# Banded attention of a two-block transformer kernel: values stationary, three heads moving, exponentials normed on GpSimd, five steps of lag

## The chip, the cores and the metric

The kernel runs on one core of a Trainium2 chip. Time is the device time of one execution in microseconds (us). The engines are TensorE (PE, with its weight loads apart as PEld), VectorE (DVE), ScalarE (ACT), GpSimd (POOL) and SyncE (SP, which only issues the loads of weights). They run side by side, each through its own instructions in their written order, and wait for each other on semaphores that the kernel sets by hand.

## The reference

Two blocks of two layers each, on 512 tokens of width 1024, in float32. The change lies in the first block, in the banded ("sliding window") attention, six query heads and two key/value heads of 64:

```python
def swa_mixer(q, k, v, q_gain, k_gain, sinks, rel_bias):
    ...
    s = jnp.einsum('bnqhgd,bnkhd->bnhgqk', qb, kb).astype(jnp.float32) * (HEAD_DIM ** -0.5)
    ...
    s = jnp.where(mask[None, :, None, None], s + bias[None, None], -jnp.inf)
    sk = sinks.astype(jnp.float32).reshape(1, 1, SWA_KV_HEADS, SWA_GROUP, 1, 1)
    lse = jnp.logaddexp(jax.nn.logsumexp(s, axis=-1, keepdims=True), sk)
    p = jnp.exp(s - lse)
    o = jnp.einsum('bnhgqk,bnkhd->bnqhgd', p.astype(v.dtype), vb)
    return o.reshape(B, S, SWA_Q_DIM)
...
        mixed = jnp.concatenate([out_a, out_b, out_c], axis=-1)
        x = x + mixed @ w_out[l]
```

A token block of 128 queries sees its own 128 keys and the 128 before (the first block only its own). `out_a` is this attention, `out_b` a pooling mixer, `out_c` full attention from latents ("mla"). The second block has two more attentions, "fox" and "nsa".

## The kernel before

Activations lie transposed (channels on partitions, 512 tokens in the row). Every weight is cut into an upper and a lower fp32r part: ACT writes the upper (`Wh`, L1520), DVE the lower by a subtraction (`Wl`, L2283), and a linear step is three 512-column matmuls (`three`, L667 to L669), called a triple here. Units of weights are cut two ahead of their use.

Each engine's program is written as one main line of linear stages and several side generators. After a piece of a linear stage the main line calls `tick()`, which lets every open side do one step. All engines make the same calls, so a step of a side stands at the same place of the main line on each. The order is the one written; nothing schedules it.

The banded attention of layer l is the side `swa_side`. It runs in the ticks of `outa{l}` (two halves of 20 ticks: five k tiles for four output tiles, one triple each). The first ticks go to the end of the mla attention, the last 32 to this side. After both halves `out0{l}` multiplies the banded output by its three k tiles; its first matmul waits for that output (`window_part`).

The 24 items are (token block t, head h), in `attend`. Of item i, step i takes the scores (two matmuls, L1209 and L1210, keys moving in 256 columns, for t = 0 in 128). On DVE one instruction adds the bias and takes the maximum (L2542), a second negates it (L2545); ACT takes the exponential with its sum (L1675). Step i + 3 turns the exponentials by PE transposes (L888), which ACT copies out (L1693). Step i + 5 mixes: the turned exponentials are the stationary tile and 64 columns of plain float32 values move (L903). After six heads of a block, DVE divides 384 columns by the sums at once (L2584), PE turns them back (L920), ACT writes the upper part `Hh` (L1582) and DVE the lower `Hl` (L2353). For the sink, DVE and ACT handle six heads in one small instruction each (L2555, L1688, L2569, L2573).

`mixing`, used by fox and nsa, is the other form. Every exponential is multiplied by its own inverted sum on GpSimd (`normalise`, L3455) before it is turned; the turned tile is split into an upper part by ACT (L1582, `PTh`) and a lower one by DVE (L2353, `PTl`); the values, upper and lower side by side in 128 columns, are stationary and several items move at once, `PTh` against both parts (L979) and `PTl` against the upper (L980). The output comes out transposed; its rows 64 to 127 have to be added to its rows 0 to 63, by an ACT copy and a DVE addition (L2081, L3123 in nsa).

PSUM has eight banks, handed out in turn by `Banks`; a new use waits until its reader has drained the last one. `outa` holds four of them. ACT runs `turn`, then `head`, then the output's copies in a step; DVE `head`, then `turn`.

Of the kernel before, what the change touches and what calls it, by code (L numbers as in the profile page):

```python
# [17 lines left out]
P = 128  # L18
S = 512
# [152 lines left out]
class Memory:  # L172


    def __init__(self, nc, ctx):
# [67 lines left out]
        self.DT = area("DT", [2, S], 19328)  # L243
        self.WSQ = area("WSQ", [2048], 6784)
# [95 lines left out]
class Signals:  # L340


    def __init__(self, nc, ctx):
# [299 lines left out]
def tensor_program(pe, M, G, K, plan):  # L643
# [225 lines left out]
    def attend(tag, items, H, scores, values, outer=True, first_mix=None, group=None):  # L869
# [73 lines left out]
    def mixing(B, scores, values, first_mix=None, group=None, extra=None, need=None, tail=6):  # L943
# [47 lines left out]
        for i in range(n + tail):  # L991
# [4 lines left out]
            c = B.ended(i - 5)  # L996
            if need and c is not None and B.closes(c) and items[i - 5][0] in PAIRS[1]:
# [36 lines left out]

    ex = Count(G.ex)
# [144 lines left out]
    for l in range(DEPTH):  # L1180
# [45 lines left out]
        def swa_values():  # L1226
            pe.wait_ge(*K.drained(f"vt{l}"))
# [274 lines left out]
def scalar_program(sc, M, G, K, plan, a):  # L1502
# [160 lines left out]
    def attend(tag, items, H, to, grouped=False):  # L1663
# [3 lines left out]
        def head(i):  # L1667
# [6 lines left out]
            if kind == "swa":  # L1674
                sc.activation(pb, pb, ACT.Exp, bias=nm, accum_out=sm).then_inc(*ex.up())  # L1675
            else:
                if i >= 4:
                    sc.wait_ge(*K.full(f"{tag} t{i - 4}"))
                sc.activation(pb, b[:, 0:w], ACT.Exp, bias=nm, accum_out=sm).then_inc(*K.empties(name))

        def turn(i):
# [3 lines left out]
            if kind == "swa" and h == H - 1:  # L1685
                x = M.STT[:, 3, t, 0:H]
                sc.wait_ge(*sink.due())
                sc.activation(x, x, ACT.Exp).then_inc(G.sink_ex, 1)  # L1688
# [1913 lines left out]
```

## Time and profile before

| | us |
|---|---|
| three runs | 2717.89, 2719.95, 2719.98 (median 2719.95) |
| the profiled execution | 2718.81 |
| its span | 2717.0 |
| PE busy | 2674.8 (98%) |
| DVE, ACT, POOL busy | 1521.7 (56%), 1135.1 (42%), 210.0 (8%) |

The span is the time from the first to the last instruction recorded; 1.8 us lie around it. The granted TensorE clock was full throughout (0.999). The chain of work that ended last lies on PE for 89% of the span and on DVE for 5%. The busy shares are averages over the whole program and say little of a stage: the banded attention stage runs from 147.6 to 195.2 us in layer 0 and from 697.6 to 745.2 us in layer 1.

### The profile page before, as it was taken

The numbers are of one execution on the slowest core, as the hardware profiler recorded it, in microseconds if no ns is written. First come the engines' busy times: TensorE is split into PE (matmuls) and PEld (weight loads), VectorE is DVE, ScalarE is ACT, GpSimd is POOL, SyncE is SP. The second block draws the span as 40 slices with busy tenths as digits, with TensorE's granted clock in tenths as the row PEclk, the third lists the DMA queues.
The fourth block names the chain that finished last, engine by engine and source line by source line (L and its number), as shares of the span: only waits on it lengthen the run. The fifth ranks groups of instructions, "written<-read, shape, count | busy, mean of one in ns | idle before, by whom it ended". The sixth has DMA issues, their size and how long they took to land.

```text
span 2717.0 us, 34704 instructions
## 1 busy us (share of the span) xinstructions
PE 2674.8 (98%) x13449; PEld 2217.3 (82%) x13449; DVE 1521.7 (56%) x2678; ACT 1135.1 (42%) x2055; POOL 210.0 (8%) x323
## 2 busy tenths in 40 slices
PE   8999999999999999999999999999999999999999
PEld 7788888887888888878877888888878778888887
DVE  7756444467564444676776653343677776643343
ACT  4644222236542222455655343242465655342232
POOL 5200000002000000021122000000020121000000
PEclk9999999999999999999999999999999999999999
DMA  5113232321132333333311333333333212323332
GB/s 146 36 42 103 93 101 93 101 81 58 34 101 96 98 97 98 93 101 89 114 48 40 98 96 93 101 94 98 109 88 105 79 40 63 104 91 101 93 101 86
DMA packets 192279, 237.70 MB, mean 87 GB/s; under 512 B 12674, under 2 KB 145764, under 8 KB 192116
## 3 DMA queue, kind: packets, MB, share of 16 engines
q1 hardware_dynamic: 188852, 228.04, 27.9%
q0 software_dynamic: 2256, 5.52, 1.0%
q8 instruction: 108, 1.77, 0.3%
q10 hardware_dynamic: 1008, 1.92, 0.2%
q14 instruction: 55, 0.45, 0.0%
HBM read 227.05 MB, written 2.11 MB: 84 GB/s over the span
## 4 chain that ended last, share of the span: by engine, by line
PE 89%; DVE 5%; ACT 2%; POOL 1%; issue 1%; DMA 0%; SPq 0%; ACTq 0%; DVEq 0%; POOLq 0%
PE bank L667 26%; PE bank L669 26%; PE bank L668 26%; PE bank L958 2%; PE bank L903 1%; PE bank L979 1%; PE bank L980 1%; PE bank L1022 1%; PE bank L1021 1%; DVE Wl L2283 1%; PE bank L1223 1%; PE bank L888 1%; PE bank L1032 1%; PE bank L1421 1%; PE bank L1017 0%
## 5 line engine op out<-in xcount | busy, mean ns | idle before, releaser
L2283 DVE TENSOR_TENSOR Wl<-RAW,Wh 128x1024 fp32r<-128x1024 f32 (+4 forms) x434 | 511.5, 1201 | 326.0 <-ACT Wh L1520 325.1
L1520 ACT ACTIVATE Wh<-RAW 128x1024 fp32r<-128x1024 f32 (+4 forms) x434 | 438.1, 1032 | 397.6 <-PE bank L669 392.4
L667 PE MATMUL bank<-Hh,Wh 128*128 128x512 f32 x1104 | 448.3, 406 | 2.2 <-DVE Hl L2353 1.5
L669 PE MATMUL bank<-Hh,Wl 128*128 128x512 f32 x1104 | 431.7, 391 | 0.0
L668 PE MATMUL bank<-Hl,Wh 128*128 128x512 f32 x1104 | 431.0, 390 | 0.0
L667 PE MATMUL bank<-HA,Wh 128*128 128x512 f32 x704 | 274.2, 390 | 0.0
L669 PE MATMUL bank<-HA,Wl 128*128 128x512 f32 x704 | 273.9, 389 | 0.0
L668 PE MATMUL bank<-HA,Wh 128*128 128x512 f32 x704 | 273.9, 389 | 0.0
L669 PEld LDWEIGHTS bank<-Hh,Wl 128*128 128x128 f32 x1104 | 207.2, 188 | 45.0
L667 PEld LDWEIGHTS bank<-Hh,Wh 128*128 128x128 f32 x1104 | 208.3, 189 | 40.6 <-issue 4.8
L668 PE MATMUL bank<-A,Wh 128*128 128x512 f32 x608 | 236.5, 389 | 0.0
L667 PE MATMUL bank<-A,Wh 128*128 128x512 f32 x608 | 236.5, 389 | 0.0
L669 PE MATMUL bank<-A,Wl 128*128 128x512 f32 x608 | 236.5, 389 | 0.0
L668 PEld LDWEIGHTS bank<-Hl,Wh 128*128 128x128 f32 x1104 | 208.1, 188 | 33.6
L669 PEld LDWEIGHTS bank<-HA,Wl 128*128 128x128 f32 x704 | 132.1, 188 | 27.5
L668 PEld LDWEIGHTS bank<-HA,Wh 128*128 128x128 f32 x704 | 132.2, 188 | 27.3
L667 PEld LDWEIGHTS bank<-HA,Wh 128*128 128x128 f32 x704 | 132.1, 188 | 27.3
L2452 DVE TENSOR_TENSOR XT<-bank,XT 128x512 f32<-128x512 f32 x112 | 77.1, 690 | 121.6 <-PE bank L669 121.0
L1738 ACT ACTIVATE P<-bank,STT 128x384 f32<-128x384 f32 (+1 forms) x192 | 101.2, 527 | 96.7 <-DVE STT L2639 95.8
L667 PE MATMUL bank<-Wh,Hh 128*128 128x512 f32 (+3 forms) x384 | 139.4, 363 | 2.2 <-DVE Wl L2283 2.2
L2353 DVE TENSOR_TENSOR A<-TMP,A 128x512 fp32r<-128x512 f32 x108 | 74.8, 693 | 117.9 <-ACT A L1933 87.2
L669 PE MATMUL bank<-Wh,Hl 128*128 128x512 f32 (+3 forms) x384 | 134.6, 350 | 0.0
(408 smaller groups left out, 4711.3 us busy)
## 6 DMA issues: line engine op xcount, KB each, us to landing
RAW<-in_w_up_dram SPq DMA_DIRECT2D x108, 512.0 KB, 3.7
RAW<-in_w_down_dram SPq DMA_DIRECT2D x108, 512.0 KB, 3.7
RAW<-in_w_in_dram SPq DMA_DIRECT2D x86, 512.0 KB, 3.7
RAW<-in_w_gate_dram SPq DMA_DIRECT2D x44, 512.0 KB, 3.7
RAW<-in_w_out_dram SPq DMA_DIRECT2D x28, 512.0 KB, 3.7
RAW<-in_cmp_w_dram SPq DMA_DIRECT2D x16, 512.0 KB, 3.9
RAW<-in_w_o_fox_dram SPq DMA_DIRECT2D x8, 512.0 KB, 4.5
RAW<-in_w_o_nsa_dram SPq DMA_DIRECT2D x8, 512.0 KB, 3.5
```

The costliest lines, as they stand in the source:

```text
L667: pe.matmul(o, sh, mh, start=first, stop=False)
L668: pe.matmul(o, sh, ml, start=False, stop=False)
L669: return pe.matmul(o, sl, mh, start=False, stop=last)
L888: x = pe.transpose(b[:, k * P:(k + 1) * P], M.PB[:, i % 4, k * P:(k + 1) * P], ident)
L903: x = pe.matmul(b[:, h * 64:(h + 1) * 64], M.PT[:, i % 3, k * P:(k + 1) * P], values(g, h, kb[k]), start=k == 0, stop=k == len(kb) - 1)
L958: x = pe.transpose(b[:, k * P:(k + 1) * P], e[:, k * P:(k + 1) * P], ident)
L979: pe.matmul(b[:, c:c + w], v, ph, start=B.opens(n) and k == 0, stop=False, skip_group_check=True)
L1520: sc.activation(M.Wh[:, v % NHL, 0:n], M.RAW[:, v % NRAW, 0:n], ACT.Copy).then_inc(G.w_hi, 1)
L1738: sc.activation(e, M.bank[K.of(name)][:, 0:e.shape[1]], ACT.Exp, bias=M.STT[:, 0, t, h:h + 1], accum_out=M.STT[:, 1, t, h:h + 1]).then_inc ...
L2283: ve.tensor_tensor(M.Wl[:, v % NRAW, 0:n], M.RAW[:, v % NRAW, 0:n], M.Wh[:, v % NHL, 0:n].bitcast(F32), ALU.subtract).then_inc(G.w_lo, 1)
L2353: return ve.tensor_tensor(lo, src, h.bitcast(F32), ALU.subtract)
L2452: ve.tensor_tensor(M.XT[:, k, :], M.bank[K.of(name)][:, :], M.XT[:, k, :], ALU.add).then_inc(*K.empties(name))
```

## The change

The banded attention leaves `attend` for `mixing`. Its items are grouped in eight trios, one (t, key/value head g) with three heads each. `mixing` gets a lag of 5 (3 elsewhere) and a tail of 8: item i is turned in step i + 5, a trio is mixed in the step i + 7 of its last item, and its finish, after the second trio of a block, is in i + 8. New operations: the upper and lower values `VS` once a layer; in each item's step the sink's exponential on ACT, the sum and its inverse on DVE, a multiplication on GpSimd, and the lower part of the turned tile on DVE; for each trio two ACT copies and two DVE additions into `OSW`, and for each block one ACT copy (`Hh`) and one DVE subtraction (`Hl`) from it. The transposes back (L920) and the division (L2584) go.

```diff
+        self.VS = area("VS", [NT, 2, P], 11904, F32R)
+        self.OSW = area("OSW", [3, S], 14976)
...
+def swa_bundles(l):
+    trios = [[(t, g, 3 * g + x) for x in range(3)] for pair in PAIRS for g in range(2) for t in pair]
+    return Bundles(f"swa{l}", trios, lambda t, g, h: f"{t}{g}", lambda t, g, h: h % 3 * P)
...
 tensor_program, mixing (scalar and vector alike)
-            if 0 <= i - 3 < n:
-                turn(i - 3)
+            if 0 <= i - lag < n:
+                turn(i - lag)
...
-            yield from attend(f"swa{l}", softmax_items(6), 6, swa_scores, lambda g, h, k: M.V1[:, k, 64 * (h // 3):64 * (h // 3) + 64],
-                              first_mix=swa_values)
+            yield from mixing(swa_bundles(l), swa_scores, lambda t, g, h, k: M.VS[:, k, g, :], swa_values, tail=8, lag=5)
...
             if k == 0:
-                for t in range(NT):
-                    pe.wait_ge(*K.drained(f"swa{l} x{t}0"))
+                pe.wait_ge(G.swa_lo, NT * l + NT)
...
 scalar_program, mixing, head
+            if banded:
+                nm = M.STT[:, 0, t, h:h + 1]
+                sc.activation(e, e, ACT.Exp, bias=nm, accum_out=M.STT[:, 1, t, h:h + 1]).then_inc(*ex.up())
+                sc.activation(M.STT[:, 3, t, h:h + 1], M.SNK[:, 6 * int(tag[3]) + h:6 * int(tag[3]) + h + 1], ACT.Exp, bias=nm).then_inc(G.sink_ex, 1)
+                return
...
+            sc.activation(M.VS[:, :, :, 0:64], M.V1[:, :, :].rearrange("p s (g d) -> p s g d", d=64), ACT.Copy).then_inc(*hi.up())
+            yield from mixing(swa_bundles(l), take=swa_take, finish=swa_out, tail=8, lag=5)
+
+        def swa_take(t, g, h):
+            o = f"swa{l} o{t}{g}"
+            sc.wait_ge(*K.full(o))
+            halves, b = trio(g, M.bank[K.of(o)])
+            for r0, x, j in halves:
+                i = sc.activation(M.OSW[r0:r0 + 64, j, t * P:(t + 1) * P], b[0:64, x, :], ACT.Copy)
+            i.then_inc(G.whole, 1)
+
+        def swa_out(t, g, h):
+            if g:
+                for x in range(2):
+                    sc.wait_ge(*K.drained(f"swa{l} o{t}{x}"))
+                sc.activation(M.Hh[:, 0:3, t * P:(t + 1) * P], M.OSW[:, :, t * P:(t + 1) * P], ACT.Copy).then_inc(*hi.up())
...
 vector_program, mixing
+            if banded:
+                if B.freed_by(i) is not None:
+                    ve.wait_ge(*K.full(f"{tag} t{B.freed_by(i)}"))
+                e, top, sk = B.exps(M, i), M.STT[:, 2, t, h:h + 1], 6 * int(tag[3]) + h
+                ve.tensor_tensor_reduce(e, M.bank[K.of(name)][:, 0:e.shape[1]], M.BIAS[:, h, (0 if t else P):256], 1.0, M.SNK[:, sk:sk + 1],
+                                        ALU.add, ALU.max, top).then_inc(*K.empties(name))
+                ve.wait_ge(*K.drained(name))
+                ve.tensor_scalar(M.STT[:, 0, t, h:h + 1], top, -1.0, None, ALU.mult).then_inc(*mx.up())
+                return
...
+            if banded:
+                total = M.STT[:, 1, t, h:h + 1]
+                ve.wait_ge(*ex.due())
+                ve.wait_ge(*sink_ex.due())
+                ve.tensor_tensor(total, total, M.STT[:, 3, t, h:h + 1], ALU.add).then_inc(*own.up())
+                ve.wait_ge(*own.now())
...
+        def swa_sum(t, g, h):
+            o = f"swa{l} o{t}{g}"
+            ve.wait_ge(*whole.due())
+            halves, b = trio(g, M.bank[K.of(o)])
+            for r0, x, j in halves:
+                y = M.OSW[r0:r0 + 64, j, t * P:(t + 1) * P]
+                i = ve.tensor_tensor(y, y, b[64:128, x, :], ALU.add)
+            i.then_inc(*K.empties(o))
+
+        def swa_out(t, g, h):
+            if g:
+                q = slice(t * P, (t + 1) * P)
+                lower(M.Hl[:, 0:3, q], M.OSW[:, :, q], M.Hh[:, 0:3, q]).then_inc(G.swa_lo, 1)
...
 gpsimd_program
+        normalise(swa_bundles(l), lambda t, g, h: M.ONE[:, 0:1])
```

DVE before, inside layer 0's stage, where the output of a block is divided (line numbers of each kernel's own; `ISA` is the bias-and-maximum instruction, its second row the read of its accumulator; `TMP`, later `P`, are the exponentials):

```order
L2542 ISA TMP_55,STT_69<-bank,BIAS_73,SS_71 128x256 [waits bank7_full,bank4_full]
L2542 ISA STT_69 128x1
L2545 TENSOR_SCALAR STT_69<-STT_69 128x1 [waits bank4_drained]
L2584 TENSOR_TENSOR OS_56<-bank,STT_69 128x384 [waits bank6_full,vector_own]
L2542 ISA TMP_55,STT_69<-bank,BIAS_73,SS_71 128x256 [waits bank7_full]
L2542 ISA STT_69 128x1
L2545 TENSOR_SCALAR STT_69<-STT_69 128x1 [waits bank7_drained]
```

DVE in the changed kernel, one step in which a trio's output is added up, and the start of the next:

```order
L2650 ISA P_9_57,STT_69<-bank,BIAS_73,SS_71 128x256 [waits bank1_full,bank3_full]
L2650 ISA STT_69 128x1
L2653 TENSOR_SCALAR STT_69<-STT_69 128x1 [waits bank3_drained]
L2663 TENSOR_TENSOR STT_69<-STT_69 128x1 [waits sink_exp_made,score_exp_made]
L2667 RECIPROCAL STT_69<-STT_69 128x1 [waits vector_own]
L2376 TENSOR_TENSOR PT_59<-bank,PT_58 128x128 [waits part_hi_made]
L3012 TENSOR_TENSOR OSW_98<-OSW_98,bank 64x128 [waits mixed_values_copied]
L3012 TENSOR_TENSOR OSW_98<-OSW_98,bank 64x2x128
L2650 ISA P_9_57,STT_69<-bank,BIAS_73,SS_71 128x256 [waits bank6_full,bank1_full]
```

Where three instructions stood for an item, six stand now, and two more for each trio behind a wait for ACT (`mixed_values_copied`).

ACT in the changed kernel, a step that takes a trio's output (copies of `OSW`) and a step with a block's `Hh`:

```order
L1740 ACTIVATE P_9_57,STT_69<-P_9_57,STT_69 128x256 [waits score_max_made]
L1741 ACTIVATE STT_69<-SS_71,STT_69 128x1
L2014 ACTIVATE OSW_98<-bank 64x128 [waits bank3_full]
L2014 ACTIVATE OSW_98<-bank 64x2x128
L1590 ACTIVATE PT_58<-bank 128x2x128 [waits bank0_full]
L1740 ACTIVATE P_9_57,STT_69<-P_9_57,STT_69 128x256 [waits score_max_made]
L1741 ACTIVATE STT_69<-SS_71,STT_69 128x1
L2021 ACTIVATE Hh_50<-OSW_98 128x3x128 [waits bank3_drained,bank6_drained]
```

The copies stand behind the exponential of the same step, which waits for DVE's maximum of that step.

PE before, the end of one item of a 256-key block and the next one's mixing:

```order
L888 MATMUL bank<-CST_61,TMP_55 128x128 [waits score_exp_made,bank6_drained]
L888 MATMUL bank<-CST_61,TMP_55 128x128
L1209 MATMUL bank<-KH_90,QP_89 128x256 [waits bank5_drained]
L1210 MATMUL bank<-KL_91,QP_89 128x256
L903 MATMUL bank<-V_36_84,TMP_55 128x64 [waits bank6_drained]
L903 MATMUL bank<-V_36_84,TMP_55 128x64
L667 MATMUL bank<-Hh_50,Wh_54 128x512
```

and in the changed kernel, a step that mixes a trio:

```order
L970 MATMUL bank<-CST_61,P_9_57 128x128 [waits score_exp_normed,bank0_drained]
L970 MATMUL bank<-CST_61,P_9_57 128x128
L1219 MATMUL bank<-KH_90,QP_89 128x256 [waits bank6_drained]
L1220 MATMUL bank<-KL_91,QP_89 128x256
L991 MATMUL bank<-PT_58,VS_97 128x384 [waits bank6_drained,bank0_drained,bank3_drained,bank1_drained]
L992 MATMUL bank<-PT_59,VS_97 64x384
L991 MATMUL bank<-PT_58,VS_97 128x384
L992 MATMUL bank<-PT_59,VS_97 64x384
L682 MATMUL bank<-Hh_50,Wh_54 128x512
```

Two steps in three have no mixing; the third has four matmuls of 384 columns.

## Rows read from the trace of the kernel before

**Rows 1.** Windows of the stage: us, busy (count) of PE, PEld, DVE, ACT, POOL, clock, DMA
```profile
147.60:153.20 5.60, 5.21 (x29) 4.11 (x28) 4.31 (x16) 2.89 (x10) 0.00 (x0) 1.00 0.13 47
153.20:185.00 31.80, 30.35 (x198) 25.56 (x198) 19.91 (x77) 19.84 (x67) 0.00 (x0) 1.00 0.13 43
185.00:195.20 10.20, 9.51 (x58) 7.83 (x56) 5.28 (x14) 4.99 (x12) 0.00 (x0) 1.00 0.09 26
...
697.60:745.20 47.60, 45.08 (x283) 37.48 (x282) 29.54 (x105) 27.73 (x88) 0.00 (x0) 1.00 0.12 40
```
**Rows 2.** Timeline of PE, one item: start, duration, what [idle before, releaser]
```profile
171.39 0.38 PE L888 MATMUL bank<-CST,TMP 128*128 128x128 f32 x2
...
171.84 0.55 PE L903 MATMUL bank<-V,TMP 128*128 128x64 f32 x4
172.21 0.47 PE L667 MATMUL bank<-Hh,Wh 128*128 128x512 f32 x1
...
172.98 0.38 PE L888 MATMUL bank<-CST,TMP 128*128 128x128 f32 x2
```
**Rows 3.** Timeline of PE, a block's output turned back, and the stage's end
```profile
191.61 0.49 PE L920 MATMUL bank<-CST,OS 128*128 128x128 f32 x3
191.85 0.47 PE L667 MATMUL bank<-Hh,Wh 128*128 128x512 f32 x1
...
195.24 0.47 PE L667 MATMUL bank<-Hh,Wh 128*128 128x512 f32 x1 [0.73 <-DVE Hl L2353]
```
**Rows 4.** Timeline of PE in fox: a 384-column fp32r matmul and the next
```profile
1181.06 0.34 PE L1022 MATMUL bank<-KAl,QA 128*128 128x384 f32 x1
1181.23 0.34 PE L1024 MATMUL bank<-CR,SEL 96*128 96x384 bf16 x1
```
**Rows 5.** Timeline of DVE in the stage: one item's head, back to back
```profile
151.55 0.48 DVE L2542 CUSTOM_DVE_ANT_0 TMP<-bank,BIAS,SS 128x256 f32<-128x256 f32 x1
...
152.07 0.15 DVE L2545 TENSOR_SCALAR STT<-STT 128x1 f32<-128x1 f32 x1
152.15 0.34 DVE L2542 CUSTOM_DVE_ANT_0 TMP<-bank,BIAS,SS 128x128 f32<-128x128 f32 x1
```
**Rows 6.** Timeline of DVE in the stage: sum and inverse
```profile
166.80 0.17 DVE L2569 TENSOR_TENSOR STT<-STT 128x6 f32<-128x6 f32 x1 [0.16 <-ACT STT L1688]
...
167.11 0.65 DVE L2283 TENSOR_TENSOR Wl<-RAW,Wh 128x512 fp32r<-128x512 f32 x1
```
**Rows 7.** Timeline of DVE in nsa: the lower part of a turned tile
```profile
1429.11 0.42 DVE L2353 TENSOR_TENSOR PT<-bank,PT 128x256 fp32r<-128x256 f32 x1 [0.57 <-ACT PT L1582]
1429.45 0.41 DVE L2639 TENSOR_REDUCE STT<-bank 128x1 f32<-128x256 f32 x1
```
**Rows 8.** Groups by line and form, DVE: count | busy, mean ns | idle before
```profile
L2452 DVE TENSOR_TENSOR XT<-bank,XT 128x512 f32<-128x512 f32 x112 | 77.1, 690 | 121.6 <-PE bank L669 121.0
...
L2353 DVE TENSOR_TENSOR PT<-bank,PT 128x128 fp32r<-128x128 f32 x48 | 13.4, 280 | 11.1 <-ACT PT L1582 11.1
```
**Rows 9.** Timeline of ACT in nsa: exponential, then an output's two copies
```profile
1418.12 0.47 ACT L1738 ACTIVATE P<-bank,STT 128x256 f32<-128x256 f32 x1 [0.35 <-DVE STT L2639]
...
1418.58 0.75 ACT L2081 ACTIVATE ONS<-bank 64x256 f32<-64x256 f32 x2
```
**Rows 10.** Timeline of DVE in nsa: the two additions behind those copies
```profile
1419.36 0.86 DVE L3123 TENSOR_TENSOR ONS<-ONS,bank 64x256 f32<-64x256 f32 x2 [1.02 <-ACT ONS L2081]
```
**Rows 11.** Timelines of POOL, then DVE, in nsa: a norming and a weight cut
```profile
1437.20 0.66 POOL L3455 TENSOR_SCALAR P<-P,STT,GS 128x384 f32<-128x384 f32 x1 [1.56 <-DVE STT L2644]
```
**Rows 12.** Timeline of DVE in nsa: two weight cuts, without and with it
```profile
1411.35 1.22 DVE L2283 TENSOR_TENSOR Wl<-RAW,Wh 128x1024 fp32r<-128x1024 f32 x1
...
1437.39 1.53 DVE L2283 TENSOR_TENSOR Wl<-RAW,Wh 128x1024 fp32r<-128x1024 f32 x1
```
**Rows 13.** Waits of the whole span: engine, line <- releaser: us, times, longest
```profile
DVE ONS L3123 <- ACT ONS L2081: 16.2, 16, 1.6
...
DVE OAl L2353 <- ACT OAh L2090: 7.4, 8, 1.0
```

More of the change, by code:

```diff
@@ L941, in attend, with mixing @@
             yield
-    def mixing(B, scores, values, first_mix=None, group=None, extra=None, need=None, tail=6):
+    def mixing(B, scores, values, first_mix=None, group=None, extra=None, need=None, tail=6, lag=3):
         tag, items = B.tag, B.items
@@ L995, in mixing @@
                 group(items[i][1])
-            c = B.ended(i - 5)
-            if need and c is not None and B.closes(c) and items[i - 5][0] in PAIRS[1]:
+            c = B.ended(i - lag - 2)
+            if need and c is not None and B.closes(c) and items[i - lag - 2][0] in PAIRS[1]:
                 while need not in done:
                     yield
-            if 0 <= i - 3 < n:
-                turn(i - 3)
+            if 0 <= i - lag < n:
+                turn(i - lag)
             if i < n:
@@ L1033, in turn_rows @@
         i.then_inc(*K.fills(name))
-    ex = Count(G.ex)
     b = fresh("first gains")
@@ L1684, in turn @@
             name = f"{tag} t{i}"
[L1685 to L1688, printed above, removed]
-            if kind == "swa" or i % 2 == 0:
+            if i % 2 == 0:
                 sc.wait_ge(*K.full(name))
@@ L1726, in attend, with mixing @@
             yield
-    def mixing(B, group=False, take=None, finish=None, need=None, tail=6):
+    def mixing(B, group=False, take=None, finish=None, need=None, tail=6, lag=3):
         tag, items = B.tag, B.items
+        banded = tag[:3] == "swa"
         def head(i):
@@ L1752, in mixing @@
                     yield
-            c = B.ended(i - 5)
-            if need and c is not None and B.closes(c) and items[i - 5][0] in PAIRS[1]:
+            c = B.ended(i - lag - 2)
+            if need and c is not None and B.closes(c) and items[i - lag - 2][0] in PAIRS[1]:
                 while need not in done:
                     yield
-            if 0 <= i - 3 < n:
-                turn(i - 3)
+            if 0 <= i - lag < n:
+                turn(i - lag)
             if i < n:
@@ L1762, in mixing @@
                 done.add(B.outs[c])
-                take(*items[i - 5])
-            c = B.ended(i - 6)
+                take(*items[i - lag - 2])
+            c = B.ended(i - lag - 3)
             if finish and c is not None and B.closes(c):
-                finish(*items[i - 6])
+                finish(*items[i - lag - 3])
             yield
@@ L2552, in turn @@
             name = f"{tag} t{i}"
-            if kind == "swa" and h == H - 1:
-                ve.wait_ge(G.mx, mx.n)
-                ve.tensor_tensor(M.STT[:, 3, t, 0:H], M.SNK[:, 6 * l:6 * l + 6], M.STT[:, 0, t, 0:H], ALU.add).then_inc(G.sink, 1)
-            if kind != "swa" and i % 2:
+            if i % 2:
                 ve.wait_ge(*K.full(name))
@@ L2566, in mix @@
                 sums = M.STT[:, 1, t, 0:H]
-                if kind == "swa":
-                    ve.wait_ge(*sink_ex.due())
-                    ve.tensor_tensor(sums, sums, M.STT[:, 3, t, 0:H], ALU.add).then_inc(*own.up())
-                    ve.wait_ge(*own.now())
-                else:
-                    ve.wait_ge(*K.drained(f"{tag} s{i + 2}"))
+                ve.wait_ge(*K.drained(f"{tag} s{i + 2}"))
                 ve.reciprocal(fac, sums).then_inc(*own.up())
@@ L2630, in attend, with mixing @@
         softmax[0] = 0
-    def mixing(B, group=False, add_up=None, finish=None, need=None, tail=6):
+    def mixing(B, group=False, add_up=None, finish=None, need=None, tail=6, lag=3):
         tag, items = B.tag, B.items
+        banded = tag[:3] == "swa"
         def head(i):
@@ L2656, in mixing @@
                     yield
-            c = B.ended(i - 5)
-            if need and c is not None and B.closes(c) and items[i - 5][0] in PAIRS[1]:
+            c = B.ended(i - lag - 2)
+            if need and c is not None and B.closes(c) and items[i - lag - 2][0] in PAIRS[1]:
                 while need not in done:
@@ L2977, in swa_side @@
                 yield
-            yield from attend(f"swa{l}", softmax_items(6), 6, (M.Hh, M.Hl, 0))
+            ve.wait_ge(*K.full(f"mla{l} t23"))
+            ve.wait_ge(*K.points[f"mla{l}", 23])
+            lower(M.VS[:, :, :, 64:128], M.V1[:, :, :].rearrange("p s (g d) -> p s g d", d=64), M.VS[:, :, :, 0:64]).then_inc(G.v_lo, 1)
+            yield from mixing(swa_bundles(l), add_up=swa_sum, finish=swa_out, tail=8, lag=5)
+        def swa_sum(t, g, h):
[10 more added lines that the diff above has]
+                lower(M.Hl[:, 0:3, q], M.OSW[:, :, q], M.Hh[:, 0:3, q]).then_inc(G.swa_lo, 1)
         swa = begin(swa_side())
```

55 lines of the change are left out of this document (23 added, 32 removed).

## The prediction

> **What bounds the kernel.** I read the windows of the banded stage first, since the shares of the whole program hide it. The stage takes 47.6 us in each layer [rows 1]; PE is busy for 45.1 of them, so PE sets its length, with DVE at 29.5 and ACT at 27.7. I split it at the places where the changed kernel differs: an opening (5.6 us, steps 0 to 4), a dense part (31.8 us, steps 5 to 23, in which an item is scored and another turned in each step) and an end (10.2 us). In the dense part DVE has 19.9 us of work in 31.8, that is 12 us of room. That room is what the change spends, so DVE's order is what has to be priced.
>
> Then the timelines, from start to start, since neighbours overlap. An item costs PE 171.39 to 172.98 = 1.59 us [rows 2]: transposes, scores, mixing (0.37), one triple.
>
> **PE, what it removes.** Mixing a wide item lasts 171.84 to 172.21 = 0.37; the six items with one key block take half, 0.18. After float32 matmuls the triple's first matmul starts late: the triple lasts 172.21 to 172.98 = 0.77 [rows 2]; where score matmuls stand ahead of it I take 0.70. So 18 x 0.37 + 6 x 0.18 + 24 x 0.07 = 9.4 us a layer. The four groups of three transposes back are 191.61 to 191.85 = 0.24 each [rows 3], 1.0 in all. Removed: 10.4.
>
> **PE, what it adds.** A 384-column fp32r matmul goes 1181.06 to 1181.23 = 0.17 after the last [rows 4]. Three token blocks with two key blocks and one with one make 7, times two trios, times two matmuls: 28 a layer, 4.8 us. PE's own work falls by 5.6 us a layer, 11.2 in both. A dense step takes PE 1.59 - 0.37 - 0.07 + 4 x 0.17 / 3 = 1.38.
>
> **DVE, an item.** The head is the same two instructions: 151.55 to 152.15 = 0.60 [rows 5]. Sum and inverse now come for each item, not for six: 166.80 to 167.11 = 0.31 [rows 6] (with one column instead of six it can be a little less, not below twice 0.08, the distance between two tiny neighbours in rows 5). The lower part of the turned tile, absent before in this stage, is 1429.11 to 1429.45 = 0.34 [rows 7]. Together 1.25 us an item, against about 0.60 before. A half-wide head or lower part is 0.42 - 0.28 = 0.14 shorter [rows 7, 8].
>
> **DVE, a trio's output.** Two additions. Rows 10 has two of 64x256 in 0.86, so 0.43 each with no overlap. The second one here is of 64x128, bounded by 0.15 (one column, rows 5) and 0.43, and taken at 0.29, nearest to the 280 ns of rows 8. Sum 0.72. The Trainium skill, "VectorE: DVE Perf Modes", section "Two Vector instructions with no wait between them", has a model by which an instruction that starts in another group of 32 partitions than the last one starts only when the earlier ones have finished. The 0.86 agrees. With the overlap of other neighbours (0.08 to 0.09) the pair would be 0.54, and the layer 1.4 us less.
>
> **The new wait.** The additions wait for ACT's copies, and ACT makes these behind the exponential of the same step, which waits for DVE's maximum. From the start of DVE's head: negation done at 0.67 (151.55 to 152.07, plus 0.15, rows 5); 0.05 to hand over; exponential with its sum 0.46 (1418.12 to 1418.58, rows 9); the sink's exponential 0.1 (not below the 0.08 of tiny neighbours, at most 0.2); copies of 64x256 and 64x128 0.38 + 0.27 (0.75 for two wide ones; the narrow one between 0.19 and 0.38); 0.05 to hand over: 1.98. DVE has done its own work at 1.25. It stands for 0.73, with everything of the next step, the next maximum too, queued behind. The trace of nsa has this very chain: copies from 1418.58 to 1419.33, the additions at 1419.36 after 1.02 us idle [rows 9, 10], and the waits list it 16 times with 16.2 us [rows 13]. With 0.72 for the work a trio's output costs DVE 1.45. The finish of a block likewise: 0.67 + 0.05 + 0.46 + 0.1 + 0.5 (an upper part of 384, estimated between the 0.38 of 256 columns and the 0.6 that 512 would take at the same slope) + 0.05 = 1.83, a stand of 0.58, then 0.47 of work: 1.05. Fox waits 7.4 us in 8 such places [rows 13].
>
> **Three steps of DVE** then take 3 x 1.25 + 1.45 = 5.2 us, 6.25 with a finish, on average 5.7, or 1.91 a step. PE wants 1.38 and had 1.59. DVE becomes the bound of the dense part.
>
> **The sum, a layer.** Dense part, 19 steps: 19 x 1.25 = 23.75, less ten half-wide heads and lower parts at 0.14 = 1.4; five outputs x 1.45 = 7.25; two finishes 2.1; four additions to XT at 0.69 - 0.09 = 0.60 [rows 8], 2.4; weight cuts, two of 1024 columns and one of 512, 2 x 1.15 + 0.57 = 2.9 (1.22 and 0.65 less the overlap; rows 12, 6). Total 37.0, against 31.8: +5.2. Opening: splitting the values (512 columns, 0.6) stands ahead of the first head on DVE and four sums and inverses are added (1.2), most of it beside PE; between 0 and +1.8, I take +0.5. End: PE has 0.5 less per step that mixed, eight steps in 8.2 us; behind the last mixing there stand copies 0.65, additions 0.75, a copy 0.5, a lower part 0.56 and hand-overs 0.3, 2.8 in a row, of which two triples cover 1.4. So 9.6 against 10.2: -0.6; the wait at `window_part` grows from 0.73 [rows 3] to about 1.4.
>
> GpSimd multiplies 24 tiles a layer at about 0.55. Item i's inverse stands in step i + 1 and its transposes in i + 5, four steps or over 6 us later, so the norming itself is hidden. But it touches DVE: the cut at 1437.39 took 1.53 instead of 1.22 beside the norming at 1437.20 [rows 11, 12]. The dense part has five DVE instructions with two SBUF inputs (three cuts, two finishes). POOL is busy a third of it; at two meetings of 0.31 this is +0.6. The Trainium skill, "GPSIMD Engine Reference", section "1. Specifications", says that GpSimd shares its SBUF interfaces with VectorE and contends with instructions of two SBUF inputs; that speaks against this change, and the last rival below is what it would make of the time.
>
> Layer: +5.2 + 0.5 - 0.6 + 0.6 = +5.7, both layers +11.4. The profiled execution took 2718.81, the median is 1.1 above it: 2718.81 + 11.4 + 1.1 = 2731.
>
> **Rivals.**
> 1. *DVE is the bound, but without standing.* If PE and ACT run far enough ahead, or the copies overlap more than I think, the seven stands a layer (5 x 0.73 + 2 x 0.58 = 4.8) vanish: +0.9 a layer, 2722. For it: nsa, with the same chain, keeps PE going. Against it: ACT cannot be ahead, its exponential needs the same step's maximum. PE's mixing is ahead of it in any case. Between this and the forecast all is possible.
> 2. *PE stays the bound* (faster). If DVE's dense step comes in under 1.38 on average, all of PE's saving shows: 5.6 a layer, and the 2.5 us that PE stands in the stage now (47.6 - 45.1, rows 1) may go too: -11 to -16, 2704 to 2709. The price list would have to be 0.5 us a step too high; halfway (1.6 a step) the kernel is faster only by the shorter end. For it: everything new is off PE, and the four banks that rotate are no longer held by long outputs. It decides from a mean DVE step of 1.5 down.
> 3. *ACT adds to it.* Its weight cuts (about as long as DVE's, rows 12) stand between exponential and copies of neighbouring steps at two places a layer; each delays an upper part and the copies behind it, which lengthens DVE's step by up to 0.8: +1.6 a layer, 2734.
> 4. *GpSimd and DVE block each other* at every chance: ten instructions of DVE with two SBUF inputs a layer meet a norming, 0.31 to 0.55 each: +2.5 to +4.9 a layer over the 0.6, 2735 to 2740.
>
> That the change doesn't do what it says I exclude: the order shows all of it.
>
> **Numbers.** Forecast (2726 to 2733) 0.45; rival 1 (2717 to 2725) 0.25; rival 2 with its halfway cases (2703 to 2716) 0.15; rivals 3 and 4 (2734 to 2742) 0.15. A measurement of this kernel tells 0.2%, 5.4 us, from no change. Faster than 2714.5: 0.13; within 2714.5 to 2725.4: 0.28; slower 0.59. The range 2712 to 2739 leaves out about 0.1 below and 0.05 above; the forecast's own range is 2726 to 2733, and both signs stay possible.
>
> **What the new profile would show.** Right: in the stage's window DVE busy over 42 us of some 53, PE's share falling to about 75%, with PE waiting at L970, L1219 or L991 for DVE's draining of banks; DVE idle before the first `OSW` addition 0.6 to 0.8 each, released by ACT; 384-column matmuls 0.17 apart; stage 53 us. Wrong: a stage below 47 us with PE over 93% busy (rival 2), or DVE without idle time ahead of `OSW` (rival 1). A wait of PE for GpSimd (L3495) over 1 us a layer would upset the place that I give the norming.

## The result, and the profile after

Four runs of the changed kernel took 2737.01 to 2741.91 us, median 2739.78, against 2719.97 us for the kernel before: a ratio of 1.0073 (95% interval 1.0061 to 1.0085), 19.8 us slower. The profiled execution took 2739.44, its span is 2737.6. I had forecast 2731, with 2739 as the end of the range: the direction was right, the size was not.

I measured the banded attention's stage from its first score matmul to the `out0` matmul that waits for its output. Before it took 47.62 us in each layer [rows 1, 3]; after, 57.40 in layer 0 and 56.55 in layer 1. These two make 18.7 of the 20.6 us by which the spans differ. Another 1.46 us lie right behind the stage of layer 0. The last 0.4 us lie ahead of it, where nothing was changed (the stage of layer 0 starts anywhere between 146.6 and 148.5 us in the kernels below, so this is scatter).

The page after, its part 1:

```profile
PE 2679.2 (98%) x13313; PEld 2214.0 (81%) x13313; DVE 1552.5 (57%) x2824; ACT 1154.3 (42%) x2129; POOL 235.9 (9%) x371
```

In these averages nearly nothing happened; the windows of the stage tell it. Since DVE turned out to set the pace, I cut the stage where DVE starts the head of item 5 and of item 23, into an opening, a middle of 18 steps and an end (columns as in rows 1). Before, layer 0:

```profile
147.62:153.84 6.22, 5.83 (x34) 4.66 (x32) 4.48 (x18) 3.52 (x12) 0.00 (x0) 1.00 0.12 42
153.84:184.30 30.46, 29.01 (x190) 24.39 (x190) 19.10 (x71) 19.06 (x64) 0.00 (x0) 1.00 0.14 45
184.30:195.24 10.94, 10.21 (x63) 8.48 (x62) 5.96 (x17) 5.16 (x13) 0.00 (x0) 1.00 0.09 24
```

After, layer 1, and the middle stretch of layer 0:

```profile
709.30:716.91 7.61, 7.09 (x38) 5.51 (x37) 6.25 (x26) 4.63 (x15) 1.67 (x3) 1.00 0.10 34
716.91:754.54 37.63, 27.40 (x133) 19.65 (x131) 29.73 (x128) 24.20 (x89) 10.03 (x19) 0.95 0.10 36
754.54:765.85 11.31, 8.97 (x47) 7.13 (x47) 9.37 (x27) 7.31 (x22) 1.53 (x3) 1.00 0.15 39
155.62:194.04 38.42, 29.70 (x133) 21.50 (x131) 29.77 (x129) 24.20 (x89) 10.05 (x19) 0.87 0.10 35
```

In layer 1 PE is busy for 27.4 of 37.6 us in the middle, DVE for 29.7. Against before, layer 1's opening is 1.39 us longer, its middle 7.17 and its end 0.37. The times in which DVE stands in that middle (releaser, us, times, longest):

```profile
DVE OSW L3012 <- ACT OSW L2014: 4.2, 5, 0.9
DVE Hl L2376 <- ACT Hh L2021: 1.5, 2, 0.8
DVE PT L2376 <- ACT PT L1590: 0.7, 2, 0.6
```

The first two kinds are the stands that I had priced; the third, for a turned upper part (`PT`), is new. One of the first kind, in the timelines of DVE and then ACT:

```profile
169.53 0.41 DVE L2376 TENSOR_TENSOR PT<-bank,PT 128x256 fp32r<-128x256 f32 x1
170.73 0.73 DVE L3012 TENSOR_TENSOR OSW<-OSW,bank 64x256 f32<-64x256 f32 x2 [0.79 <-ACT OSW L2014]
```

```profile
169.36 0.51 ACT L1740 ACTIVATE P<-P,STT 128x256 f32<-128x256 f32 x1 [0.85 <-DVE STT L2653]
169.78 0.19 ACT L1740 ACTIVATION_READ_ACCUMULATOR P<-P,STT 128x1 f32 x1
169.87 0.28 ACT L1741 ACTIVATE STT<-SS,STT 128x1 f32<-128x1 f32 x1
170.05 0.64 ACT L2014 ACTIVATE OSW<-bank 64x256 f32<-64x256 f32 x2
```

ACT waits for DVE's maximum, then DVE waits for ACT's copies. Exponential and sink take 169.36 to 170.05 = 0.69, where the sum of the prediction has 0.46 + 0.1.

The end of the stage in layer 1, DVE and then PE (for comparison with the second part of [rows 3]):

```profile
761.85 0.68 DVE L2475 TENSOR_TENSOR XT<-bank,XT 128x512 f32<-128x512 f32 x1
762.46 0.68 DVE L2306 TENSOR_TENSOR Wl<-RAW,Wh 128x512 fp32r<-128x512 f32 x1
763.05 0.68 DVE L2475 TENSOR_TENSOR XT<-bank,XT 128x512 f32<-128x512 f32 x1
763.77 0.73 DVE L3012 TENSOR_TENSOR OSW<-OSW,bank 64x128 f32<-64x128 f32 x2
764.52 0.69 DVE L2475 TENSOR_TENSOR XT<-bank,XT 128x512 f32<-128x512 f32 x1
765.14 0.56 DVE L2376 TENSOR_TENSOR Hl<-OSW,Hh 128x384 fp32r<-128x384 f32 x1
```

```profile
765.85 0.47 PE L682 MATMUL bank<-Hh,Wh 128*128 128x512 f32 x1 [2.20 <-DVE Hl L2376]
```

The last additions have no idle time ahead of them: DVE's own cut and additions to `XT` stand in front of them.

One thing I had not thought of at all is in the clock column. The granted TensorE clock, full throughout before, is at its lower level (1.2 of 2.4 GHz) for some stretches: 13.6 us in and right behind the stage of layer 0, 3.4 us in that of layer 1 (added up from windows of 0.5 us). Two windows of 3 us in layer 0, right after PE stood 1.9 us for DVE up to 181.24 and 2.2 us up to 205.41, and one at the same place of layer 1, after the 2.20 us up to 765.85:

```profile
181.00:184.00 3.00, 2.76 (x9) 2.27 (x10) 2.02 (x9) 1.99 (x9) 1.07 (x2) 0.54 0.01 3
205.00:208.00 3.00, 2.59 (x6) 2.15 (x7) 2.60 (x4) 1.14 (x2) 0.00 (x0) 0.53 0.43 148
766.00:769.00 3.00, 3.00 (x14) 2.49 (x15) 2.04 (x3) 0.58 (x2) 0.00 (x0) 1.00 0.28 98
```

So the same stand is followed by the lower clock in one layer and by the full clock in the other; in these traces the drops go with PE's standing, but the length of one stand doesn't tell whether one comes. The second window lies right behind the final wait, where PE is the bound again, and there the lower clock is paid in full: from the `out0` matmul to a common place in the next stage it is 31.19 us before and 32.65 after, the 1.46 us named above.

### The profile page after: what moved, and what is told of

The parts are those of the page before. It is cut to its first block, busy times and chain, and to the rows that moved or that the text cites. A ratio compares the mean times of both kernels' runs of the same rounds, so it can differ in the third digit from the quotient of the medians.

```text
span 2737.6 us, 34752 instructions
## 1 busy us (share of the span) xinstructions
PE 2679.2 (98%) x13313; PEld 2214.0 (81%) x13313; DVE 1552.5 (57%) x2824; ACT 1154.3 (42%) x2129; POOL 235.9 (9%) x371
## 4 chain that ended last, share of the span: by engine, by line
PE 88%; DVE 6%; ACT 2%; issue 1%; POOL 1%; DMA 0%; ACTq 0%; DVEq 0%; POOLq 0%
PE bank L682 26%; PE bank L684 25%; PE bank L683 25%; PE bank L970 2%; PE bank L991 1%; DVE Wl L2306 1%; PE bank L992 1%; PE bank L1033 1%; PE bank L1034 1%; PE bank L915 1%; PE bank L1233 1%; PE bank L1044 1%; PE bank L1429 1%; PE bank L1029 0%; DVE STT L2655 0%
## 5 line engine op out<-in xcount | busy, mean ns | idle before, releaser
L2376 DVE TENSOR_TENSOR PT<-bank,PT 128x384 fp32r<-128x384 f32 (+3 forms) x240 | 110.2, 459 | 46.9 <-ACT PT L1590 46.1
```

Source lines behind the costliest of these rows:

```text
L2376: return ve.tensor_tensor(lo, src, h.bitcast(F32), ALU.subtract)
```

## Experiments

All are edits of the changed kernel, timed beside the kernel before. The 95% interval of a ratio is some 0.1% to each side, so medians that lie less than some 3 us apart tell little, and the stage in the trace of one profiled execution decides there.

| kernel | us | ratio to before (interval) | stage, layers 0 and 1 |
|---|---|---|---|
| before | 2719.97 | | 47.62, 47.62 |
| changed | 2739.78 | 1.0073 (1.0061 to 1.0085) | 57.40, 56.55 |
| take_first | 2732.31 | 1.0044 (1.0030 to 1.0057) | 53.33, 52.27 |
| lag3 | 2740.43 | 1.0076 (1.0063 to 1.0088) | 56.84, 57.76 |
| pool_sums | 2737.00 | 1.0062 (1.0050 to 1.0075) | 54.62, 55.14 |
| direct | 2730.33 | 1.0041 (1.0029 to 1.0054) | 54.58, 53.19 |
| direct_first | 2725.12 | 1.0021 (1.0012 to 1.0030) | 50.67, 50.60 |
| combo | 2719.89 | 1.0002 (0.9993 to 1.0011) | 48.00, 47.92 |
| dve_light | 2716.59 | 0.9989 (0.9980 to 0.9998) | 46.27, 46.22 |
| warm | 2740.36 | 1.0075 (1.0062 to 1.0087) | 57.54, 57.56 |
| vs_pool | 2739.20 | 1.0073 (1.0059 to 1.0087) | 56.32, 56.71 |
| more_dve | 2751.22 | 1.0114 (1.0100 to 1.0128) | 62.98, 61.96 |
| combo_vs | 2718.31 | 0.9995 (0.9986 to 1.0004) | 47.32, 47.29 |
| combo_lag4 | 2723.48 | 1.0014 (1.0005 to 1.0023) | 49.19, 50.78 |

**The stands (take_first).** On ScalarE the head, with its exponential, moves behind the copies:

```diff
+            if banded:
+                if 0 <= i - lag < n:
+                    turn(i - lag)
+                if c is not None and B.closes(c):
+                    done.add(B.outs[c])
+                    take(*items[i - lag - 2])
+                c = B.ended(i - lag - 3)
+                if c is not None and B.closes(c):
+                    finish(*items[i - lag - 3])
+                if i < n:
+                    head(i)
+                yield
+                continue
```

> One edit on ScalarE alone: in a step of the banded attention the two copies of a trio's output and the block's upper part stand ahead of the exponential, not behind it. Theory 1 (VectorE bounds the stage and stands for ScalarE): the trace after has five stands ahead of the OSW additions in the dense part of a layer (0.83, 0.79, 0.94, 0.80, 0.80 us) and two ahead of Hl (0.80, 0.67), 5.6 us a layer. They go, the stage shortens by about 5 us, and with two layers the kernel takes 2728 to 2731 instead of 2739.8. Theory 2 (the stands are only the far side of a loop through PE, and the exponential, now 0.7 us later, makes the next sum wait instead): under 2 us in all, 2737 to 2741. Theory 3 (most of what the forecast missed is TensorE's half clock, set off by PE standing): the half-clock stretches, 17 us of the stage of layer 0 after, stay, and the time stays within 2 us.

Measured 2732.3: 7.5 us less, a little short of theory 1's 9 to 12 and far from theories 2 and 3. (That text puts the lower clock at 17 us of the stage of layer 0; the trace has 10.2 there, 3.4 right behind it and 3.4 in layer 1.) DVE's waits in the middle stretch of layer 1, by the same view:

```profile
DVE OSW L3025 <- ACT OSW L2027: 0.8, 3, 0.3
DVE PT L2389 <- ACT PT L1590: 0.6, 1, 0.6
```

4.9 of the 5.7 us of stands for `OSW` and `Hl` are gone, and the stretch is 4.3 shorter (33.36). The stands are on the path.

**DVE's work, more and less (more_dve, pool_sums).**

```diff
+            ve.reciprocal(M.STT[:, 2, t, h:h + 1], M.STT[:, 1, t, h:h + 1]).then_inc(*own.up())
+            ve.wait_ge(*own.now())
... the same two lines once more ...
             ve.reciprocal(M.STT[:, 4, t, h:h + 1], M.STT[:, 1, t, h:h + 1]).then_inc(*rec.up())
```

> The changed kernel with the inverse of an item's sum taken three times on VectorE, one after the other: two instructions of 128x1 more an item, each waiting for the last, about 0.19 us each, 0.38 an item, 9.1 us a layer. Theory 1 (VectorE's own sequence bounds the stage; its standing for ScalarE is part of a loop that begins with its own head, so work behind the head is partly taken out of the standing): the stage grows by 0.38 in the steps without a stand and by nothing in the seven with one, 16 x 0.38 = 6 us a layer, 2750 to 2754. Theory 2 (VectorE's work bounds without a loop): all of it, 2756 to 2759. Theory 3 (ScalarE or PE bounds): under 6 us, below 2746.

```diff
 vector_program, invert: a banded item has nothing left to do
 gpsimd_program, normalise, banded
...
+                gp.tensor_tensor(total, total, M.STT[:, 3, t, h:h + 1], ALU.add).then_inc(*own.up())
...
+                gp.tensor_tensor(M.STT[:, 4, t, h:h + 1], total, M.LV[:, 0:1], ALU.pow).then_inc(*own.up())
```

> The changed kernel with the sum (with the sink) and its inverse made on GpSimd (an addition and a power of -1, 128x1 each) instead of VectorE. Theory 1 (VectorE bounds the stage): sum and inverse take 172.09 to 172.37, 0.28 us a step, in 19 dense steps 5.3 us a layer, 10.6 in both; the stands stay; 2728 to 2731. Theory 2 (what bounds is the standing for ScalarE, and VectorE then just stands longer): under 3 us, 2737 to 2740. Theory 3 (GpSimd's two small instructions are slow and make it the bound): slower than 2740, with PE waiting for L3495's norming.

More work cost 11.4 us, theory 1 of its text. DVE's waits in the middle stretch of layer 1 say why it isn't the 18 us that were added:

```profile
DVE OSW L3017 <- ACT OSW L2014: 2.5, 5, 0.7
DVE Hl L2376 <- ACT Hh L2021: 0.7, 2, 0.4
```

Of 18 x 0.38 = 6.8 us added there, 2.5 were taken out of these two kinds of stand, the third kind (0.7) is gone too, and the stretch grew by 3.9 (37.63 to 41.52).

Less work gave 2.8 us (theory 2), a difference that the two medians alone don't make sure. The waits in the middle of layer 1 show the same loop from its other side:

```profile
DVE OSW L3007 <- ACT OSW L2014: 4.7, 5, 1.2
DVE PT L2376 <- ACT PT L1590: 3.0, 4, 1.1
DVE Hl L2376 <- ACT Hh L2021: 2.0, 2, 1.1
```

DVE now arrives earlier and stands for ScalarE's upper part of the turned tile: 9.7 us of stands where there were 6.4. So in the steps with an output the bound is neither DVE's work nor the waits alone but the loop DVE's maximum, ACT's exponential, ACT's copies, DVE's additions. The stretches say where the gain came from. The opening, which has no output to add up yet, got 1.22 and 1.24 us shorter (6.39 and 6.37). The middle, where 18 x 0.28 = 5.0 us of work were taken away, is 36.93 in layer 0 at the full clock, 0.7 under the 37.63 that the changed kernel takes there at the full clock (warm, below), and 37.46 in layer 1 at a clock of 0.86.

**Nothing to add up (direct), and together (direct_first, combo).** PE, then ScalarE and VectorE of a trio's output:

```diff
+                    pe.matmul(b[0:64, c:c + w], v[:, 0:64], ph, start=k == 0, stop=False, ...)
+                    pe.matmul(b[0:64, c:c + w], v[:, 64:128], ph, start=False, stop=False, ...)
...
+                i = sc.activation(M.Hh[r0:r0 + 64, j, t * P:(t + 1) * P], b[0:64, x, :], ACT.Copy)
...
+                i = ve.tensor_tensor(M.Hl[r0:r0 + 64, j, q], b[0:64, x, :], M.Hh[r0:r0 + 64, j, q].bitcast(F32), ALU.subtract)
```

> The changed kernel with the output mixed by three matmuls into the same 64 rows (values' upper and lower part against the upper exponentials, upper values against the lower ones), so that there is nothing to add up: ScalarE writes the upper part Hh and VectorE the lower part Hl straight from PSUM, OSW and the block's finish go. PE gets 14 more 384-column matmuls a layer, 2.4 us. Theory 1 (VectorE bounds, and the end of the stage is a chain behind the last mixing): VectorE loses four finishes of 0.48 and two stands of 0.7 in the dense part, the end loses the copy 0.5, the lower part 0.56 and hand-overs: 3 to 4 us a layer, 2731 to 2734. Theory 2 (PE or its clock bounds): the 2.4 us on PE show, 2740 to 2745.

> The two edits that helped, together: three matmuls into the same 64 rows (ScalarE writes Hh, VectorE writes Hl from PSUM), and on ScalarE these copies ahead of the exponential. Alone they took 9 and 7 us off the changed kernel. Theory 1 (VectorE bounds; what remains in 'three matmuls' are its 6.3 us of stands a layer for ScalarE's Hh): half or more of these go, 2721 to 2726. Theory 2 (both edits remove the same stands, and PE with 2.4 us more work a layer is near its bound): 2727 to 2730.

> The same two edits and the sums with their inverses on GpSimd as well. Theory 1 (VectorE's work bounds once it no longer stands): the 0.28 us a step that gave only 2.8 us with the stands in place now show fully, 19 steps x 0.28 x 2 = 10 us below the kernel with the first two edits, bounded by PE's own step (1.38 + 4 x 0.17 / 2 / 3, about 1.5 us against 1.6 for VectorE): 2714 to 2720. Theory 2 (ScalarE's turned upper part or GpSimd's longer chain is next): no more than 3 us below the kernel with the two edits.

direct gave 9.5 us, a little more than theory 1 has, although PE got 2.4 us more a layer; the final wait fell from 2.2 to 0.7. Of the 9.1 us between the two profiled executions 6.2 lie in the stages. Another 1.5 us lie behind that of layer 0, where the clock stays full now, and 1.4 ahead of it, the scatter of its start.

direct_first (2725.1) is theory 1: DVE's stands for ScalarE in the middle of layer 1 fall from direct's 4.9 us to 2.3. combo (2719.9) lies at the upper end of theory 1's range, but its mechanism isn't borne out: the sums and inverses, 10 us in the middle stretches (36 x 0.28), don't show fully. The gain is 5.2 us, and nearly half of it is the opening's (1.24 and 1.22 us). Windows of the middle: pool_sums in layer 0, then direct_first and combo in layer 1:

```profile
153.36:190.29 36.93, 27.41 (x139) 19.04 (x137) 26.24 (x93) 24.38 (x91) 26.35 (x61) 1.00 0.12 36
708.33:740.55 32.22, 25.96 (x141) 19.18 (x139) 28.28 (x127) 23.29 (x87) 10.09 (x19) 1.00 0.12 42
704.20:734.99 30.79, 26.91 (x147) 19.84 (x145) 24.62 (x91) 23.44 (x89) 26.80 (x61) 1.00 0.13 44
```

The middle gives 1.4 us a layer for the 5.0 taken off DVE, against 0.7 with the stands in place. Here too most turns into standing: DVE waits 5.2 us for ScalarE in combo's stretch, 2.3 in direct_first's. The three edits together bring the stage back to about the length that it had before, not below it.

**What PE's side is worth (dve_light).** take_first and pool_sums together, and:

```diff
-            lower(B.turned(M.PTl, i), ..., B.turned(M.PTh, i))
+            w = 8 if banded else P
+            lower(B.turned(M.PTl, i)[:, :, 0:w], ..., B.turned(M.PTh, i)[:, :, 0:w])
...
-                y = M.OSW[r0:r0 + 64, j, t * P:(t + 1) * P]
+                y = M.OSW[r0:r0 + 64, j, t * P:t * P + 8]
```

> What PE's side of the change is worth by itself: the changed kernel with ScalarE's copies first and sums on GpSimd, and with VectorE's new work cut to 8 columns (lower part of the turned tile, additions of an output); the matmuls with the lower part read the upper part instead, so the number of PE's instructions stays. It leaves out part of the computation (128 columns of each of these become 8). Theory 1 (PE's saving is real and VectorE hides it): the stage of 47.6 us falls by the 5.6 us a layer that I counted, perhaps 1 more or 2 less: 2706 to 2713. Theory 2 (PE gains nothing even without VectorE, because five steps of lag, four banks or the half clock hold it): 2717 or more.

2716.6, between its theories. The stage's window in layer 1:

```profile
696.82:743.04 46.22, 40.63 (x216) 30.85 (x214) 32.11 (x131) 35.14 (x123) 32.30 (x72) 1.00 0.14 42
```

PE has 40.6 us of work against 45.0 before: 4.4 saved in busy time, not 5.6. It stands for 5.6 us, against 2.6 before, 1.6 of them at `out0`. Of the saving 1.4 us a layer reach the time, with DVE busy for 32.1 us against 29.5 before. What holds the rest back isn't taken apart. The trace names DVE's draining of banks (1.8 us in all) and one norming on GpSimd (1.1 us) as what PE waits for ahead of the final wait, and DVE itself stands 7.0 us there for ScalarE's upper parts.

**The clock (warm).**

```diff
             b = fresh(f"{tag} t{i}")
+            if tag[:3] == "swa":
+                for _ in range(1):
+                    pe.matmul(b[:, :], M.KH[:, 0, 0:P], M.QP[:, 0, :], start=True, stop=True, ...)
             pe.wait_ge(*norm.due())
```

> The changed kernel with one 512-column matmul more in each turning step of the banded attention, into the bank that the transposes then overwrite, 24 a layer, 0.23 us each: 5.5 us a layer of PE work that nothing reads. PE stands for 12 us in that stage. Theory 1 (PE has room, and its standing is what drops the granted clock to half for 17 us in layer 0 after the change): the half-clock stretches shrink and the time is 0 to 3 us lower, 2736 to 2740. Theory 2 (PE is on the path often enough): slower by 2 to 8 us, 2742 to 2748, whatever the clock does.

2740.4, the same as without. Whole stages of warm, and then of the changed kernel:

```profile
147.82:205.36 57.54, 46.93 (x239) 36.01 (x238) 45.59 (x179) 36.03 (x123) 13.21 (x24) 1.00 0.11 34
709.37:766.93 57.56, 46.98 (x239) 36.04 (x238) 45.38 (x179) 36.04 (x123) 13.19 (x24) 1.00 0.11 35
```

```profile
148.01:205.41 57.40, 45.83 (x215) 34.16 (x214) 45.56 (x179) 36.12 (x123) 13.25 (x24) 0.91 0.11 36
709.30:765.85 56.55, 43.47 (x216) 32.29 (x214) 45.36 (x179) 36.14 (x123) 13.22 (x24) 0.97 0.11 36
```

With PE kept at work the clock stays up inside both stages. The 11 us of PE work (48 x 0.23) cost nothing in the middle stretch (37.63 and 37.66 against 38.42 and 37.63) and 1.0 us in each end, where PE is close to the bound. Both layers now agree in the middle, so the 0.8 us by which layer 0 was longer are the half clock's. But behind the stage of layer 0, after a stand of 1.95 us at `out0`, the clock falls in warm too, and the way to layer 1's stage is as long as in the changed kernel (504.0 and 503.9 us, 502.4 before):

```profile
207.00:210.00 3.00, 3.00 (x9) 2.32 (x8) 0.55 (x1) 0.00 (x0) 0.00 (x0) 0.50 0.00 0
```

The price of the half clock in the changed kernel is then about 0.8 + 1.46 = 2.3 us in the profiled execution. The four runs point the same way: mean granted clocks of 0.998, 0.995, 0.995, 0.993 go with 2737.01, 2739.44, 2740.12 and 2741.91.

**The opening (vs_pool, combo_vs).** The lower part of `VS` moves from DVE to GpSimd:

```diff
-            lower(M.VS[:, :, :, 64:128], ...).then_inc(G.v_lo, 1)
+        gp.tensor_tensor(M.VS[:, :, :, 64:128], v1, M.VS[:, :, :, 0:64].bitcast(F32), ALU.subtract).then_inc(G.v_lo, 1)
```

> The changed kernel with the lower part of the values VS (0.62 us of VectorE, once a layer, ahead of the first head) made on GpSimd, which is idle there. It asks whether VectorE's work in the opening has cover. Theory 1 (VectorE is behind from the opening on, so nothing there is covered, and my +0.5 for the opening should have been near its upper bound): the stage shortens by 0.5 to 0.7 us in each layer, 2738 to 2739 in all. Theory 2 (the opening has slack, as the forecast had it): the stage stays within 0.2 us.

> The best version so far (three matmuls into the same rows, copies ahead of the exponential, sums on GpSimd: 2719.9) with the lower part of the values on GpSimd too. Theory 1 (VectorE behind from the opening on, here too): 0.4 to 0.6 us a layer less, 2718.5 to 2719.3. Theory 2 (GpSimd, busy 26.6 of 30.6 us in the dense part, is late with its first items): no gain or a loss, 2720 to 2722.

In vs_pool the opening shortens from 7.61 to 7.00 in both layers, all that was taken off DVE. The median hardly moves (2739.2, just outside theory 1). In layer 1 the middle stretch gives the gain back, at a lower clock than the 0.95 of the changed kernel:

```profile
715.12:753.53 38.41, 29.68 (x133) 21.53 (x131) 29.85 (x128) 24.17 (x89) 10.00 (x19) 0.87 0.12 35
```

In combo, where the clock stays full, the same move takes 0.68 and 0.63 us off the stages and 1.6 off the median. pool_sums and combo add the other half: without the sums and inverses the opening is 1.2 us shorter. DVE's work in the opening has no cover. combo_vs is the fastest of those that leave nothing out, 0.05% under the kernel before, and its interval includes no difference at all.

**The lag (lag3, combo_lag4).** `tail=6, lag=3` in place of `tail=8, lag=5`, and `tail=6, lag=4` in combo_vs.

> The changed kernel with a lag of 3 steps between scores and turning instead of 5 (all engines alike, tail 6). Theory 1 (VectorE bounds the dense part, the lag matters only at the end): PE mixes the last trio two steps earlier, VectorE's backlog is the same, so the final wait of 2.2 us before the out0 matmul shrinks by 0.5 to 1.4 a layer: 2737 to 2739. Theory 2 (the lag of five is what hides GpSimd): the turned item would stand for the norm; each step gets longer by 0.2 or more on PE, the kernel is slower, 2743 or more.

> The same as the run before it with a lag of 4 steps instead of 5. Theory 1 (the last output is mixed one step earlier and PE is the bound at the end): up to 0.7 us a layer less, 2717.5 to 2719. Theory 2 (GpSimd now needs 1.3 us an item and PE turns it a step earlier: PE stands for the norm): 1 to 4 us more, 2720 to 2724.

lag3 is as fast as lag 5 (2740.4), between its two theories. PE's waits in the stage of layer 1:

```profile
PE bank L970 <- POOL P L3495: 7.7, 7, 2.0
```

With five steps there is no such wait. The waits cost less than their sum, since DVE is the bound: opening and middle grow by 0.8 and 2.9 us, and the end falls from 11.31 to 8.78, without a wait at `out0`. Both theories were half right. In combo_vs, where GpSimd also makes the sums, a step less cost 5.2 us. That lies in theory 2's range, but PE stands for GpSimd only 0.4 us in the stage of layer 1. Opening and middle are 1.1 and 1.0 us longer in each layer, with a stand of 3.0 us for DVE's lower parts against 1.4, and in layer 1 the end takes 12.16 us at a clock of 0.86 where layer 0 has 10.54 at the full clock. Why a step less lengthens the opening and the middle stays open.

## Why the prediction was wrong in size

**What held.** DVE is the bound of the dense part and PE waits for it, at the places that were named. DVE is busy for 45.4 us of layer 1's stage (forecast over 42) and PE for 77% (75%). The 384-column matmuls stand 0.17 apart. A wide item costs DVE 1.20 (1.25). A trio's two additions take 0.76 start to start (162.85 to 163.61; the forecast has 0.72); the 0.54 with overlap is excluded. The Trainium skill, "VectorE: DVE Perf Modes", section "Two Vector instructions with no wait between them", has a model that lets an instruction in another group of 32 partitions start only when the earlier ones have finished. The 0.76 agrees. PE never waits for GpSimd at a lag of five in this stage.

**The middle: mechanism right, size short.** In the 18 steps DVE's work with its gaps is 37.63 - 6.4 = 31.2; the terms of the sum without the stands, for one step less, give 31.0. The stands are what was mis-sized: 6.4 against 4.8. The five before the additions are 0.79 to 0.94 each (forecast 0.73), the two before `Hl` 0.80 and 0.67 (0.58); exponential and sink, 0.69 and not 0.56, are the step of that chain that was too short. Another 0.7 are stands for a turned upper part behind ACT's weight cut, which is rival 3, smaller than priced. GpSimd's +0.6 did not come. Together the middle is 1.3 a layer over the forecast.

**GpSimd and DVE.** Of DVE's weight cuts in the middle only the one of 512 columns meets a norming, once a layer, and it kept its length. GpSimd's instruction is what got longer:

```profile
172.55 1.09 POOL L3495 TENSOR_SCALAR P<-P,STT,ONE 128x256 f32<-128x256 f32 x1 [2.39 <-DVE STT L2667]
```

```profile
172.69 0.68 DVE L2306 TENSOR_TENSOR Wl<-RAW,Wh 128x512 fp32r<-128x512 f32 x1
```

It took 1.09 instead of 0.56 (1.09 at 733.83 in layer 1 too), beside a cut that took its usual 0.68. The Trainium skill, "GPSIMD Engine Reference", section "1. Specifications", says that GpSimd shares its SBUF interfaces with VectorE and contends with instructions of two SBUF inputs. This cut has two, and the 1.09 agrees; but here GpSimd pays, and four steps of slack hide it. Rival 4 fell.

**The step that failed.** "Opening ... most of it beside PE; between 0 and +1.8, I take +0.5" and "End: PE has 0.5 less per step that mixed ... -0.6". Both priced the two ends of the stage as PE's. In the opening that gave DVE's new work, 0.6 for the values and 1.2 for four sums and inverses, a cover that wasn't there. DVE starts head 5 2.2 us behind PE's first score matmul for it (155.62 against 153.43; before, 0.5: 153.84 against 153.38), and what it does in the opening it carries through the stage. The opening grew by 1.39, near the bound of 1.8 that I had set aside; vs_pool and combo_vs give the 0.6 of the values back us for us, pool_sums and combo the 1.2 of the sums. The end was +0.37 instead of -0.6. When PE has taken its last scores (752.32) DVE has two heads to do yet (753.34 and 754.54), and the last additions wait behind DVE's own cut and `XT` addition (2.2 us at `out0`, where the forecast has 1.4). Opening and end together are 1.9 a layer over the forecast.

**What was missing.** The half clock, about 2.3 us, for which the sum has no term. The ledger of the profiled execution, both layers: forecast 11.4; the middle's stands, less the 0.6 for GpSimd, 2.6; opening and end 3.8; clock 2.3; scatter ahead of the stage 0.4. That is 20.5 of the 20.6 us by which the spans differ. All of these terms are read from one execution of each kernel.

**Rivals.** Rival 1 (no stands) fell: they are there, and take_first shows them on the path. Rival 2 asked for all of PE's saving, which the prediction puts at 5.6 us a layer: dve_light shows 4.4 of busy time, and 1.4 a layer in the stage.

## What to carry to other kernels

When a change moves the bound from one engine to another, price every part of the stage, its opening and end too, by the new bound's sequence: cover that the old bound gave is gone from the first step in which the new one is late. Where engine A waits for B's copy behind an instruction of B that waits for A's result, put the copies ahead of it on B; here that one reordering gave 7.5 us. A saving of work on one side of such a loop is mostly turned into standing: 5.0 us taken off DVE gave 0.7 us in the middle stretch with the stands in place and 1.4 with most of them gone, while the same move in the opening, outside the loop, came through whole.

## What was unexpected of the hardware

- In a stage where TensorE stood for DVE again and again, up to 2.2 us at a time, its clock was granted at the lower level for 13.6 us around layer 0 and 3.4 in layer 1; matmuls of 512 columns then started 0.43 apart instead of 0.23. After a stand of 2.2 us ahead of `out0` the clock fell in layer 0 and stayed full in layer 1. It costs where PE is the bound right after (1.46 us behind layer 0's stage). 24 idle matmuls a layer kept it up inside the stage, at 1.0 us in each end, but not behind the final wait of layer 0.
- On GpSimd a power of -1 on 128x1 took 0.55 us, as long as the multiplication of 128x256 beside it; the addition of 128x1 took 0.19.
- A GpSimd multiplication of 128x256 went from 0.56 to 1.09 us beside a DVE cut of 512 columns, and the cut kept its 0.68. In nsa, before the change, it was the cut that got longer (1.53 for 1.22, rows 12).
